# One layer of a two-branch decoder: the next head pair's projections one block earlier, its splits one place up, its stacks sent in the odd head

## What is computed

```python
h = x @ W_in + b_in        # splits into q/k/v of 8 stick-breaking heads, q/k/v and a forget
                           # logit of 8 forgetting heads, and two 1024-wide branch gates
# branch A, stick-breaking (sb): z = q k^T / 8, weights = exp(log_sigmoid(z) + suffix sum of log_sigmoid(-z))
# branch B, forgetting (fx):     z = q k^T / 8 + c_q - c_k, softmax over the causal part
merged = sigmoid(g_sb) * (o_sb @ W_proj_sb) + sigmoid(g_fx) * (o_fx @ W_proj_fox)
x = layer_norm(alpha * x + merged @ W_out)
# then a gated convolution block (x @ W_up, conv, gelu, @ W_down) and a second layer_norm
```

## Time and profile before

| | |
|---|---|
| median of 3 runs | 751.29 us (751.28 to 751.56) |
| the profiled execution | 749.84 us, its span 748.0 us |
| TensorE busy | 738.1 us, 99% of the span |
| VectorE, ScalarE, GpSimd busy | 367.9, 319.3 and 337.8 us |
| chain that ended last | 88% TensorE, 6% VectorE, 2% ScalarE, 1% DMA |
| attention stage | about 79 to 290 us |

### The profile page before, as it was taken

How to read it: one execution, slowest core, us unless ns; L and a number is a source line. 1 busy time by engine, 2 the same in 40 slices (tenths; PEclk the granted TensorE clock), 3 DMA queues, 4 the chain that set the end, 5 groups by cost and what they waited for, 6 DMA issues and landing times.

```text
span 748.0 us, 9555 instructions
## 1 busy us (share of the span) xinstructions
PE 738.1 (99%) x3483; PEld 616.6 (82%) x3483; DVE 367.9 (49%) x558; ACT 319.3 (43%) x429; POOL 337.8 (45%) x245
## 2 busy tenths in 40 slices
PE   9999999999999999999999999999999999999995
PEld 6888888888888888888898888888888888888884
DVE  3439679889789764455642211221221122322567
ACT  4322684875775775751123322333233233423410
POOL 6654344433424444981015454544444452755800
PEclk9999999999999999999999999999999999999999
DMA  9223413315124214670004233232323227232002
GB/s 316 95 92 119 128 57 112 86 58 141 58 85 113 85 57 160 234 252 29 1 1 137 88 95 101 87 110 84 112 84 103 94 94 292 92 112 84 29 28 85
DMA packets 24478, 78.34 MB, mean 105 GB/s; under 512 B 2944, under 2 KB 3328, under 8 KB 24448
## 3 DMA queue, kind: packets, MB, share of 16 engines
q1 hardware_dynamic: 24448, 77.94, 31.5%
HBM read 71.63 MB, written 2.10 MB: 99 GB/s over the span
## 4 chain that ended last, share of the span: by engine, by line
PE 88%; DVE 6%; ACT 2%; issue 2%; DMA 1%; SPq 0%; DVEq 0%; ACTq 0%
PE ps L1005 86%; PE ps L1102 1%; DVE sb_t L817 1%; DVE fx_p L808 1%; DMA fx_k<-k_bias_rows 1%; DVE sb_t L848 1%; DVE sb_k L772 0%; ACT sb_hi L586 0%; DVE fx_p L845 0%; PE ps L1184 0%; DMA w_raw<-w_stream_in 0%; DVE fx_lo L703 0%; DVE fx_k L703 0%; DVE q_bias_rows L762 0%; ACT w_hi L480 0%
## 5 line engine op out<-in xcount | busy, mean ns | idle before, releaser
L418 POOL TENSOR_TENSOR w_lo<-w_raw,w_hi 128x512 fp32r<-128x512 f32 x220 | 294.9, 1362 | 368.5 <-ACT w_hi L480 363.0
L480 ACT ACTIVATE w_hi<-w_raw 128x1024 fp32r<-128x1024 f32 x109 | 115.3, 1058 | 219.8 <-DMA w_raw<-w_stream_in 219.7
L1005 PE MATMUL ps<-x1T_hi,w_hi 128*128 128x512 f32 (+1 forms) x376 | 141.3, 376 | 0.0
L1005 PE MATMUL ps<-x1T_lo,w_hi 128*128 128x512 f32 (+1 forms) x376 | 141.2, 375 | 0.0
L1005 PE MATMUL ps<-x1T_hi,w_lo 128*128 128x512 f32 (+1 forms) x376 | 141.2, 375 | 0.0
L968 DVE SCALAR_TENSOR_TENSOR conv<-ps,col,conv 128x511 f32<-128x511 f32 (+1 forms) x44 | 33.0, 749 | 166.8 <-ACT conv L666 163.8
L1005 PE MATMUL ps<-xT_hi,w_hi 128*128 128x512 f32 x264 | 105.2, 398 | 0.0
L1005 PE MATMUL ps<-xT_hi,w_lo 128*128 128x512 f32 x264 | 103.1, 390 | 0.0
L1005 PE MATMUL ps<-xT_lo,w_hi 128*128 128x512 f32 x264 | 103.0, 390 | 0.0
L1005 PEld LDWEIGHTS ps<-x1T_lo,w_hi 128*128 128x128 f32 x376 | 70.8, 188 | 12.9
L1005 PEld LDWEIGHTS ps<-x1T_hi,w_hi 128*128 128x128 f32 x376 | 70.8, 188 | 12.9
(11 more groups left out here) (148 smaller groups left out, 1129.8 us busy)
## 6 DMA issues: line engine op xcount, KB each, us to landing
w_raw<-w_stream_in SPq DMA_DIRECT2D x109, 512.0 KB, 3.3
wout_raw<-w_out_in SPq DMA_DIRECT2D x8, 512.0 KB, 5.2
r_raw<-w_stream_in SPq DMA_DIRECT2D x5, 512.0 KB, 9.0
xT_raw<-xT_in SPq DMA_DIRECT2D x8, 256.0 KB, 6.7
x<-x_tok_in SPq DMA_DIRECT2D x4, 512.0 KB, 4.2
ln_rows<-rows_in SPq DMA_DIRECT2D x4, 512.0 KB, 5.8
out_dram<-x SPq DMA_DIRECT2D x8, 256.0 KB, 2.1
sb_q<-sb_q SPq DMA_DIRECT2D x8, 128.0 KB, 2.3
```

The costliest lines, as they stand in the source:

```text
L418: lo = nc.gpsimd.tensor_tensor(w_lo[:, slot, cs], w_raw[:, slot, cs], plain(w_hi[:, slot, cs]), ALU.subtract)
L480: nc.scalar.activation(w_hi[:, slot, :], w_raw[:, slot, :], ACT.Copy).then_inc(hi_ready, 1)
L1005: return nc.tensor.matmul(out_, lhs, rhs, start=start, stop=stop, skip_group_check=True)
```

## The change

Three things are done, all for the pairs 1 to 3 (prepared in the heads 0 to 5). Every instruction stays the same; only places in the orders move.

The fill: an even head had gate, gate, qk 0 and has gate, qk 0, qk 1; an odd head had qk 1, 2, 3, gate and has qk 2, 3, gate, gate. VectorE: split 1 moves ahead of `fx_lo`, and split 3 ahead of `sb_lo`. SyncE: stack(1) moves from the even head, behind its first weight load, to the odd head, behind its last.

```diff
         if h >= HALVES - 2:
             kinds = ["gate"] * (3 + h % 2)
         else:
-            kinds = [1, 2, 3, "gate"] if h % 2 else ["gate", "gate", 0]
+            kinds = [2, 3, "gate", "gate"] if h % 2 else ["gate", 0, 1]
...
-                    if h % 2 == 0 and k == 0:
-
-                        sp.wait_ge(qk_split, pair * 4 + 4)
+                    if h == 0 and k == 0:
+                        sp.wait_ge(qk_split, 4)
                         stack(1)
-                    if h % 2 == 1 and h < TAIL and k == 2:
-                        sp.wait_ge(qk_split, pair * 4 + 2)
-                        stack(0)
+                    if h % 2 == 1 and h < TAIL and k >= 2:
+                        sp.wait_ge(qk_split, pair * 4 + 2 * (k - 1))
+                        stack(k - 2)
...
                 split_next(h, 0)
+                split_next(h, 1)
 
                 dve.wait_ge(fx_w_hi, h + 1)
                 split_lo(fx_lo[:], ps[:, FX_PS:FX_PS + FLAT], fx_hi[:]).then_inc(fx_w_split, 1)
-                split_next(h, 1)
                 split_next(h, 2)
+                split_next(h, 3)
 
                 dve.wait_ge(sb_w_hi, h + 1)
                 split_lo(sb_lo[:], ps[:, SB_PS:SB_PS + FLAT], sb_hi[:]).then_inc(sb_w_split, 1)
-                split_next(h, 3)
```

## The result

The change makes the kernel slower. The changed kernel takes **760.19 us** (median of 4 runs, 759.83 to 760.49), the kernel before 751.42 (4 runs, 751.28 to 751.68): a ratio of 1.0117, 95% interval 1.0105 to 1.0129. The forecast was 761.9 in a range of 756.0 to 765.5. The profiled execution took 759.83 us with a span of 758.0, against 749.84 and 748.0.

A forecast was written before the change was run, and what follows sets the result against it. TensorE, busy 738.1 of 748.0 us, was taken to bound the kernel. Per odd head 2.16 + 1.7 - 0.32 = 3.54 us, 10.6 for three, took 749.84 to 760.4; adding 1.45 gave 761.9 us, range 756.0 to 765.5.

The forecast's parts named there:

- Bound and direction: Whole kernel: only TensorE's waits move the end; the change can win at most 0.95 us; slower 0.93.
- the seams' waits: TensorE between the heads of two pairs waits for `fx_k` (stack(1)); about 0.32 us each, 0.95 in three, would go.
- Part 1: Odd heads, before k = 2: TensorE waits for ScalarE's read of qk 2, held by split 0; 2.16 us, bounds 2.16 and 2.93.
- What stands behind the read on ScalarE: Odd heads: `w_hi`, sb Exp, `fx_hi` and the read of qk 3 come later but stay hidden, costing nothing.
- Part 2: Odd heads, before the sb output: `sb_lo`, behind splits 2 and 3 slowed by GpSimd, makes TensorE wait; 1.7 us taken.
- the choice of 1.7: TensorE's wait for `sb_lo`: 1.7 us taken, between 1.5 from the plain sum and 1.9 from the walk.
- the walk operation by operation: VectorE gets in one operation after each GpSimd instruction; `sb_lo` ends at 132.8, a wait of 1.9 us.
- Rival D: TensorE's waits make its clock fall, costing 1.8 us per head, 5.4 in all: 767.3 us; chance 0.05.
- the second waits: TensorE's waits for `sb_lo` before the sb output in the odd heads; 1.7 us each.
- The sum: Heads 1, 3 and 5: 2.16 + 1.7 - 0.32 = 3.54 us each, 10.6 together.
- the first waits: TensorE's waits before k = 2 in the odd heads, for the read of qk 2; 2.16 us each.
- The offset: Whole kernel: the median stands 1.45 us above the profiled execution, turning 760.4 into 761.9.

The follow-up runs named there:

- the two kernels that remove two or all of them: Kernel before with split 1 ahead of `fx_lo` and the odd heads' third `w_hi` behind `sb_hi`, without and with stack(1)'s new place: 749.81 and 749.77 us.
- the one with zero low parts: Changed kernel, GpSimd writing zeros instead of subtracting for the two weight blocks made during splits 2 and 3 of heads 1, 3, 5: 757.67 us, ratio 1.0065.

## Why the prediction was right, and where it was not

**Bound and direction: right.** TensorE waits where it did not; the seams' waits went (0.23). That 0.95 us was all there was to win holds for the first profile of the kernel before; in its second the same three seams hold 1.42 us, and the two kernels that remove two or all of them gained 1.6 us between the medians (by the intervals 0.8 to 2.6 and 1.1 to 2.5). The bound was read from one execution and was too low; the forecast used it only as 0.32 a head.

**Part 1, right by its own steps.** `select_bias` fell from 1.26 to 0.49 as its GpSimd neighbour moved away, the read started 0.09 behind split 0, and the wait is 2.11 to 2.14 where 2.16 was forecast. Giving qk 2 its own place removes it; waiting one split longer lengthens it by 2.3, the split's length. That the `w_lo` must leave for `select_bias` to be fast is shown the other way too: in the kernel with its own place for qk 2, a `w_lo` ran from 114.16 and `select_bias` took 1.25 again. What stands behind the read on ScalarE (sb Exp, `fx_hi`, read of qk 3) did not hold TensorE up, as forecast.

**Part 2, right mechanism, mis-sized term.** The plain sum (splits 8.6, `sb_lo` at 132.4, wait 1.5) was nearly exact: 8.5, 132.45 and 1.37. The step that failed is the choice of 1.7, halfway to the walk operation by operation, which put `sb_lo` at 132.8. The last two operations of split 3 ran free (1.39), since GpSimd was done at 128.79.

**Rival D, the clock: argued away wrongly.** I held that a fall behind 4.8 us of standing still spoke against one behind 2.2. Rows 9 show only that 4.8 is enough, not how little is. It fell in head 3 of the changed kernel, behind 2.14 us. Its price there, 1.64, is close to the 1.8 forecast, in part by luck: the forecast took eight matmuls at twice the time from the program's start, and in head 3 eight starts, from 174.57 to 177.95, are 0.42 us apart. The row at the start does not show a low clock, since the windows over it give 1.00. But D's time, 767.3, added the falls to the second waits, and a fall swallows that wait: net it costs 1.64 - 1.37 = 0.27 us in this kernel. This fits that the executions agree within 0.7 us although their mean granted clocks are 0.996, 0.994, 0.992 and 0.992 (0.998 before), which by my estimate from the one fall profiled would be one to three falls each. Had split 3 not been in the way, each fall would have counted in full, as the profile with split 3 put back shows (7.19 instead of 5.57, and no second wait to take it up). The executions of that kernel and of the one with zero low parts lie 2.4 and 3.3 us apart, the fastest of each at the highest mean clock (0.997); four executions each are few.

**The sum.** Forecast 10.6, measured 9.8 in the stretch: the second wait is 0.33 smaller in two heads and replaced by a fall that is 0.06 smaller in the third, which makes 0.7; the first waits make the other 0.1. That head 3 costs what was forecast is luck: its 1.64 us are not the forecast second wait but the fall that the forecast had put at nothing. **The offset:** I added 1.45 for the distance between the profiled execution and the median. Between the medians the difference is 8.8 (7.9 to 9.7 by the interval). The second profile of the kernel before makes it likely that the first was one with an early start; the 1.45 belongs to that execution, not to the kernel, and after's profiled execution stood only 0.36 under its median. Which share of the remaining 1 us is the start and which the seams stays open.

## What to carry to other kernels

Moving work earlier in an order pays only if what frees its buffer moves with it: here the read of a block moved up by three operations, its split stayed, and the engine that sets the end waited for the difference. When two engines slow each other, moving one operation moves the other's work as well, so ask under which operation it comes to lie; the same move of one `w_hi` gave -0.23% together with split 1's new place and +0.24% without it. And a new wait of TensorE of about 2 us should be costed with a fall of the clock as an even chance (6 of 12 here), one of 4.4 us with a fall as good as certain (3 of 3), less what a later wait would have cost anyway.

## What the runs showed of the hardware

- The granted clock can fall to 0.50 behind waits of only 2.1 us, and did in 6 of 12. In head 3 of the changed kernel it then stood at 0.50 for about 3.4 us; behind waits of 2.1 and 2.7 us a fall cost 1.55 to 1.67 us. With waits of 4.4 us it fell all three times, at 1.55 to 2.76. No wait of 1.64 us or less had a fall behind it.
- Where both have work, VectorE and GpSimd take turns: two subtractions of 64 x 512 took 3.36 us instead of 1.39 beside three GpSimd instructions. `sb_lo`, with one input in PSUM, was 1.49 with and without GpSimd beside it. The Trainium skill, page "SBUF — State Buffer", section "Who interferes with whom", says that the port pair the two engines share is an exclusive lock, that a VectorE instruction with two inputs in SBUF contends with a GpSimd instruction that reads SBUF, and that one with at most one input in SBUF, outside the two-port modes, does not. The trace agrees: single subtractions took 1.66 and 1.69 us beside GpSimd and 0.69 alone, and `sb_lo` did not change.
- SyncE's issue of one stack DMA took 1.31 us where its neighbours took 0.47 and 0.60, and that one seam became 1.31 from start to start. Three other profiles have such an issue among the four of this stack in head 1 (1.12, 1.40 and 1.69 us); what makes it slow no run shows. From the chain of the kernel with split 1 moved:

```profile
130.34 0.47 SPq L345
...
130.85 1.31 SPq L346
...
132.20 0.60 SPq L345
```
